# Start addresses of the operands of the halves products: 64-byte steps or 256-byte steps

## What is computed

```python
h = rms_norm(x, g_mix)
A, B, C, D = split(h @ w_in)              # w_in: 2048 x 4392
x += concat(attention of the four groups) @ w_out
x += square(relu(rms_norm(x, g_mlp) @ w_up)) @ w_down   # 2048 -> 8192 -> 2048
x += (ple @ w_ple) * sigmoid(rms_norm(x, g_ple) @ w_ple_gate)
```

## Time and profile before

| | |
|---|---|
| median of 3 runs | 3658.19 us (3654.46 to 3667.28) |
| the profiled execution's own time | 3663.53 us |
| its span in the profile | 3661.7 us |
| PE busy | 3414.7 us, 93% |
| DVE, ACT, POOL busy | 39%, 31%, 52% |
| mean granted TensorE clock | 0.951 of full speed |
| DMA | 453 MB, 124 GB/s in the mean |

### The profile page before, as it was taken

How to read it: one execution, slowest core, us unless ns; L and a number is a source line. 1 busy time by engine, 2 the same in 40 slices (tenths; PEclk the granted TensorE clock), 3 DMA queues, 4 the chain that set the end, 5 groups by cost and what they waited for, 6 DMA issues and landing times.

```text
span 3661.7 us, 58682 instructions
## 1 busy us (share of the span) xinstructions
PE 3414.7 (93%) x20676; PEld 3069.6 (84%) x20676; DVE 1432.6 (39%) x2291; ACT 1124.3 (31%) x1614; POOL 1899.1 (52%) x1189
## 2 busy tenths in 40 slices
PE   7998988899999999998989998888999999999988
PEld 5676755599999999998967776556999999999988
DVE  5334544474042240426352345344730423304263
ACT  2333322233333333332333332222333333333322
POOL 4554200067666676676565541001676676666664
PEclk9999988899999999999989999888999999999999
DMA  5333412144454444443343333221444444444433
GB/s 166 104 110 100 122 52 67 56 138 150 144 150 150 141 153 145 147 153 138 117 130 103 118 89 107 57 67 64 139 153 139 150 152 143 150 144 150 150 121 121
DMA packets 295722, 453.09 MB, mean 124 GB/s; under 512 B 36336, under 2 KB 111344, under 8 KB 294832
## 3 DMA queue, kind: packets, MB, share of 16 engines
q1 hardware_dynamic: 295328, 448.66, 38.9%
q0 software_dynamic: 144, 0.87, 0.1%
HBM read 435.54 MB, written 14.06 MB: 123 GB/s over the span
## 4 chain that ended last, share of the span: by engine, by line
PE 83%; DVE 8%; issue 5%; ACT 2%; DMA 1%; SPq 0%; POOL 0%; DVEq 0%; ACTq 0%; POOLq 0%
PE ps L687 18%; PE ps L686 18%; PE ps L685 18%; PE ps L743 5%; PE ps L780 4%; PE ps L746 4%; PE ps L768 4%; PE ps L745 3%; PE ps L849 2%; DMA ring<-in_w_in 1%; DVE ssq L1333 1%; PE ps L884 1%; ACT prob L1110 1%; PE ps L818 1%; DVE xhi L1283 1%
## 5 line engine op out<-in xcount | busy, mean ns | idle before, releaser
L649 POOL TENSOR_TENSOR wlo<-ring,whi 128x1024 fp32r<-128x1024 f32 x600 | 1479.1, 2467 | 1326.6 <-ACT whi L1095 1326.6
L1095 ACT ACTIVATE whi<-ring 128x1024 fp32r<-128x1024 f32 x600 | 635.1, 1060 | 1431.8 <-PE ps L687 1431.8
L685 PE MATMUL ps<-xhi,wlo 128*128 128x320 f32 x2560 | 802.7, 314 | 23.1 <-issue 19.9
L686 PE MATMUL ps<-xlo,whi 128*128 128x320 f32 x2560 | 797.6, 312 | 0.0
L687 PE MATMUL ps<-xhi,whi 128*128 128x320 f32 x2560 | 797.5, 312 | 0.0
L685 PE MATMUL ps<-hhi,wlo 128*128 128x320 f32 x2176 | 661.9, 304 | 15.7 <-DVE hhi L1603 9.9
L687 PE MATMUL ps<-hhi,whi 128*128 128x320 f32 x2176 | 674.6, 310 | 0.0
L686 PE MATMUL ps<-hlo,whi 128*128 128x320 f32 x2176 | 671.9, 309 | 0.0
L636 POOL TENSOR_TENSOR rlo<-ring,whi 128x256 fp32r<-128x256 f32 (+2 forms) x576 | 416.3, 755 | 392.5 <-ACT whi L1079 392.1
L685 PEld LDWEIGHTS ps<-xhi,wlo 128*128 128x128 f32 x2560 | 486.8, 190 | 28.4 <-issue 26.7
L686 PEld LDWEIGHTS ps<-xlo,whi 128*128 128x128 f32 x2560 | 487.1, 190 | 1.0 <-issue 0.4
(11 more groups left out here) (239 smaller groups left out, 3227.4 us busy)
## 6 DMA issues: line engine op xcount, KB each, us to landing
ring<-in_w_up SPq DMA_DIRECT2D x256, 512.0 KB, 3.7
ring<-in_w_down SPq DMA_DIRECT2D x256, 512.0 KB, 3.5
ring<-in_w_in SPq DMA_DIRECT2D x120, 512.0 KB, 3.5
ring<-in_w_out SPq DMA_DIRECT2D x64, 512.0 KB, 4.0
ring<-in_w_ple_gate SPq DMA_DIRECT2D x64, 512.0 KB, 3.5
xsave<-x SPq DMA_DIRECT2D x8, 640.0 KB, 7.4
x<-xsave SPq DMA_DIRECT2D x8, 640.0 KB, 5.2
ring<-in_w_in SPq DMA_DIRECT2D x16, 288.0 KB, 2.8
```

What stands on the lines that cost most here:

```text
L649: nc.gpsimd.tensor_tensor(wlo[:, s, :], ring[:, s, :], whi[:, s, :].bitcast(f32), ALU.subtract)\
L685: mm(out, lo[:, k, cols], xh, start=start, stop=False)
L686: mm(out, hi[:, k, cols], xl, start=False, stop=False)
L1095: A(whi[:, s, :], ring[:, s, :], ACT.Copy).then_inc(hi_ready, 1)
```

## The change

It does three things.

1. The first buffer starts at a multiple of 256 bytes, not of 64.
2. `arena`/`hlo`, `proj_ac`, `t0`, `t1`, `pleh` and `plel` are placed before `table` and the small buffers. With this every buffer that is an operand of a halves product starts at a multiple of 256 bytes.
3. In the chunks of w_in that are 264 and 288 columns wide, the second block of 128 rows lies 320 columns behind the first, not 264 or 288. The DMA, ScalarE's copy, GpSimd's subtraction and TensorE's reads take that pitch.

The start addresses, modulo 256 bytes, that follow:

| operand | before | after |
|---|---|---|
| `xhi`, `xlo`, `hhi`, `whi`, `wlo`, `rlo`, `xw`, `xv` | 128 | 0 |
| `hlo` | 64 | 0 |
| `pleh`, `plel` | 160 | 0 |
| second block of a 264-column unit in `whi`, `rlo` | 160 | 0 |
| second block of a 288-column unit in `whi`, `rlo` | 0 | 0 |

Within a buffer the steps are multiples of 256 bytes both before and after: a block of 320 tokens is 1280 bytes, one of `xw` 1536, of `xv` 1024, the stationary operand steps by 512.

```diff
-        top = [nc.sbuf_base + (-nc.sbuf_base) % 64]
+        top = [nc.sbuf_base + (-nc.sbuf_base) % 256]
...
         whi = sb("whi", [128, RING, 1024], f32r)
+        at = top[0]
+        arena = sb("arena", [128, KB * TOK])
+        hlo = sb("hlo", [128, KB, TOK], f32r, at)
...
+        at = top[0]
+        proj_ac = sb("proj_ac", [128, 3, 768], at=at)
+        t0 = sb("t0", [128, 2, TOK])
+        t1 = sb("t1", [128, 2, TOK])
+        pleh = sb("pleh", [128, 2, TOK], f32r)
+        plel = sb("plel", [128, 2, TOK], f32r)
         table = sb("table", [128, T_END])
...
+        PITCH = {512: 512, 256: 256, 264: 320, 288: 320}
...
-                    dst = dst.rearrange("p (a n) -> p a n", a=src.shape[1])
+                    dst = dst.rearrange("p (a n) -> p a n", a=src.shape[1])[:, :, 0:src.shape[2]]
...
-                    for c in range(0, cols, LO_COLS):
-                        w = min(LO_COLS, cols - c)
+                    w = ncol if ncol < 2 * LO_COLS else LO_COLS
+                    for c in [a * PITCH[ncol] + b for a in range(nk) for b in range(0, ncol, w)]:
...
-                hi, lo = (w[:, n % RING, 0:nk * ncol].rearrange("p (a n) -> p a n", a=nk) for w in (whi, rlo))
+                hi, lo = (w[:, n % RING, 0:nk * PITCH[ncol]].rearrange("p (a n) -> p a n", a=nk)[:, :, 0:ncol]
+                          for w in (whi, rlo))
...
-                    A(whi[:, s, 0:nk * ncol], ring[:, s, 0:nk * ncol], ACT.Copy).then_inc(hi_ready, 1)
+                    dst, src = (w[:, s, 0:nk * PITCH[ncol]].rearrange("p (a n) -> p a n", a=nk)[:, :, 0:ncol]
+                                for w in (whi, ring))
+                    A(dst, src, ACT.Copy).then_inc(hi_ready, 1)
```

More of the change, by code:

```diff
@@ L114, in build @@
         whi = sb("whi", [128, RING, 1024], f32r)
+        at = top[0]
+        arena = sb("arena", [128, KB * TOK])
+        hlo = sb("hlo", [128, KB, TOK], f32r, at)
+        proj_d = arena[:, 0:3 * 1544].rearrange("p (t n) -> p t n", t=3)
+        plout = arena[:, :].rearrange("p (b n) -> p b n", b=KB)
+        at = top[0]
[4 more added lines that the diff above has]
+        plel = sb("plel", [128, 2, TOK], f32r)
         table = sb("table", [128, T_END])
@@ L119, in build @@
         eps = sb("eps", [128, 1])
[L120 to L124, removed]
         otok = sb("otok", [128, 3, 256])
@@ L142, in build @@
         acc = sb("acc", [128, TOK + 64])
[L143 to L148, removed]
         cqT_pad = cqT[:, 3 * TOK:]
@@ L583, in _ @@
                     src = I["w_in"][l, rows[0]:rows[0] + rows[1], cols[0]:cols[0] + cols[1]]
-                    load(l, i // RING, i % RING, nk * cols[1], src.rearrange("(a p) n -> p a n", p=128))
+                    load(l, i // RING, i % RING, nk * PITCH[ncol], src.rearrange("(a p) n -> p a n", p=128))
                 for c in range(4):
@@ L628, in _, with lower_in_place @@
             with pool.Fori(0, DEPTH) as l:
-                def lower_in_place(n, cols):
+                def lower_in_place(n, nk, ncol):
                     s = n % RING
                     hold(hi_ready, l * HL + n + 1)
-                    for c in range(0, cols, LO_COLS):
-                        w = min(LO_COLS, cols - c)
+                    w = ncol if ncol < 2 * LO_COLS else LO_COLS
+                    for c in [a * PITCH[ncol] + b for a in range(nk) for b in range(0, ncol, w)]:
                         last = nc.gpsimd.tensor_tensor(rlo[:, s, c:c + w], ring[:, s, c:c + w],
@@ L641, in _ @@
                     _, _, nk, ncol, _ = CHUNK_AT[STREAM[n][0]]
-                    lower_in_place(n, nk * ncol)
+                    lower_in_place(n, nk, ncol)
                 hold(proj_copied, (l + 1) * N_WIN)
```

## The result

The changed kernel takes **3675.48 us** (median of 9 runs, 3660.82 to 3687.7) against 3658.19 us before (9 runs, 3641.78 to 3669.2): ratio 1.0047, 95% interval 1.0028 to 1.0065, so 10 to 24 us slower. The forecast was 3506 us, with a range from 3450 to 3668. The value of rival B was 3672.

The account below looks back on a forecast made before the run. TensorE was taken to bound the kernel. Savings of 81 (up, gate), 51 (down), 6 (w_out, w_ple) and 13 us (w_in) sum to 151: 3663.5 to 3512, about 5.3 lower for the median, 3506 us; range 3450 to 3668.

Parts of the forecast that it names:

- rival B: Down product: moving `hlo` off 64 loses its cheaper pace, 2.3 ns a matmul, 14 us slower, 3672 us; chance 0.12.
- What bounds the kernel: Whole kernel: TensorE is busy 3414.7 of 3661.7 us, so nearly every nanosecond off these products' matmuls shortens it.
- the excess: f32r matmuls at the higher clock: time beyond their columns, 13.3 ns or 32 clocks in up, paid once a matmul.
- The plain f32 rows: Plain f32 matmuls of 512 columns in two passes: 429.3 ns for 426.7, an excess of only 2.6 ns.
- after the change both are whole lines: Halves products: stationary and moving operands fill whole 256-byte lines, so 320 columns fall from 146.7 to 135.9 ns.
- 81 us of up and gate: Up and gate products: 7680 matmuls gain 10.8 ns each, 98% at the higher clock, 81 us.
- 6 us of w_out and w_ple: Last blocks of w_out and w_ple: 576 matmuls at 146.9 ns gain 10.8 ns each, 6 us.
- 13 us of w_in: w_in: 26 us from shorter matmuls, counted half since PE may only wait longer for the softmax, 13 us.
- the mechanism: f32r operand reads: SBUF is read in 256-byte lines and partial lines cost time; forecast 3506 us, chance 0.50.
- The down product: Down product: 6144 matmuls fall from 144.4 to 135.9 ns, 98% at the higher clock, 51 us saved.
- The pitch: 264- and 288-column units of w_in: the 320-column pitch changes pieces on POOL, off the chain; counted as nothing.
- Rival C: Halves products: one of two read paths gains, excess falls from 32 to 16 clocks, 75 us, 3583 us; chance 0.07.

Follow-up runs that it names:

- e7: Changed kernel with `hlo` and `xlo` both at 64 bytes past a multiple of 256, all else at multiples of 256: 3656.61 us, ratio 0.9997 to the kernel before.
- e5: Kernel before with `xlo` moved from 128 to 64 bytes past a multiple of 256: 3648.69 us, ratio 0.9972.
- e8: Kernel before with only the 320-column pitch of the 264- and 288-column units, no buffer moved: 3655.81 us, ratio 1.0001.
- e4: Kernel before with `xlo` moved from 128 to 192 bytes past a multiple of 256: 3648.31 us, ratio 0.9971.
- e6: Kernel before with `xlo` moved from 128 to 160 bytes past a multiple of 256: 3645.2 us, ratio 0.9961.
- e9: Same program as e6 (kernel before, `xlo` at 160), measured again in more rounds: 3644.47 us, ratio 0.998.
- m1: Separate kernel of 24-matmul f32r streams, 64 pairs of operand starts, also triples and zero data: 146.3 to 147.3 ns a matmul across the pairs.
- e3: Kernel before without the relu's lower bound, so no zeros in the down product's moving operand: one run, 3648.82 us, down at 144.4 ns.

## Why the prediction was wrong

- **What bounds the kernel** was right: PE, at the distance of starts. And the reading of the excess was right as far as the rows went: about 32 clocks a matmul whatever its columns, only at the higher clock. The plain f32 rows were misread: L833 makes 7 products of 512 columns, and the trace has 14 matmuls for them, so a plain f32 product takes two instructions of 429.3 ns, each two passes long, and not one. The excess of 2.6 ns is that of one such instruction.
- **The step that failed** is "after the change both are whole lines", with its price 146.7 to 135.9 ns. The streams show 146.7 ns with both operands at multiples of 256, as with the other 63 pairs. The 81 us of up and gate and the 6 us of w_out and w_ple were 0, and the 13 us of w_in less than 1. The price itself, the 2.6 ns of the f32 row, no f32r matmul of 320 columns showed in any run. I had the argument against it in hand (four moving starts at one price) and gave the mechanism half of the chances since no row showed the one pair that was left. Where four values of an input give one answer, a fifth that is special needs a reason from a row; mine came from how a port might work.
- **The down product**: predicted -51 us, measured +2.3 ns a matmul. 6144 of them, 98% at the higher clock, are +14 us, and the runs say 10 to 24. That is rival B, place, price and sign. Its reason, a read that falls between those of the weights, no run shows; a price for the offset alone, as B has it, is refuted by `e7`, where `hlo` is at 64 and down ran at 442 in five rounds.
- **B's chance of 0.12** was too low because of the row that I held against it: w_out's blocks, same buffers, same starts, 146.9 ns. That row is one stretch of w_out. The last unit of the same product, in the same trace (28 starts), runs at the distance of the down product:

```profile
764.28 0.30 PE L685 MATMUL ps<-hhi,wlo 128*128 128x320 f32 x1
...
768.18 0.30 PE L685 MATMUL ps<-hhi,wlo 128*128 128x320 f32 x1
```

3.90 us over 27, 144.4 ns. And in `e5`, which doesn't touch these buffers, most of w_out ran so. So w_out too has both rhythms, and the counter-argument was a window taken for a product.

- **The pitch** at nothing: right (`e8`, 1.0001).
- **The range** reached to 3668, 0.3% above the time before, and left out the one rival that lay beyond it.
- **Rival C's sum** has a slip. 14,400 x 6.7 ns are 96 us, down already has 14 of them, and at 98% this gives 81 us and 3577 us, not 75 and 3583. Nothing hangs on it.
- By the 16-byte lines of the Trainium skill (SBUF — State Buffer, Specifications (TRN2)) a start at any multiple of 32 bytes streams alike, and the streams of one placement agree: 146.3 to 147.3 ns in all 64 pairs. The rule doesn't foresee the triples, which differ with the halves' starts. The Trainium skill's rule of N/2.4 + 2.5 ns (TensorE: Matmul & The Clock Gate, Back-to-back issue gap), by which 135.8 ns would have been within reach, is given there for a matmul without its weight load; no f32r stream here came near it at 320 columns.

## What to carry to other kernels

Read the distance between starts at full clock, per product, before and after, and in more than one place: it showed in two rows what took nine runs to show in time, since the runs of one kernel spread over 27 us (at granted clocks from 0.949 to 0.958). Don't round buffers up to a large power of two in the hope of speed; here it put all operands at the same start, and with equal starts every stream of f32r triples settled at 440 ns. Another start for the buffer that is used once in three can gain, but of 56 such placements 13 ended lower, 35 the same and 8 higher, so check the whole kernel: the streams didn't foretell its rhythm (`e4`, `e6`, `e7`), and one profiled execution doesn't stand for the next (`e6` and `e9`).

## What was not expected of the hardware

- A chain of f32r matmuls at the higher clock can repeat in several rhythms, 1040, 1048, 1056 or 1072 clocks a triple of 960 columns among them, or 3184 for three triples, and stays in one for a hundred microseconds and more (each down round of 110 us). Where one plain f32 matmul stood in the stream, the rhythm was another one behind it in 30 of 48 up rounds. The same code and addresses took 144.4 ns a matmul in three rounds of a loop and 146.7 in the fourth.
- What remains open is what the 32 clocks are. They are not the start addresses (`m1`), not the data (`m1`, `e3`); at half the clock they are absent, for plain f32 nearly so the earlier trace rows. No experiment here changed the size or the order of the weight loads in a steady stream, so a cost of the f32r weight load is neither shown nor excluded.
